# The first mixer's units in another order, with its output units begun on half of the tokens

## The reference, cut to what matters

```python
def retention_gla_mixer(h, w_in, ret_theta, gla_gk_w, gla_gk_b, gla_norm_g, s0):
    qa, ka, va, ga, qb, kb, vb, gb, lr = split_cols(h @ w_in, EVEN_SPLITS)
    ...                     # decays: from ret_theta for a, from lr for b
    o_a, ra_f, ra_b = bidir_scan(qa, ka, va, la_f, la_b, s0[0], s0[1])
    y_a = silu(ga) * merge_heads(rms_norm(o_a))
    o_b, sb_f, sb_b = bidir_scan(qb, kb, vb, ...)
    y_b = silu(gb) * merge_heads(rms_norm(o_b, gla_norm_g))
    return concatenate([y_a, y_b], axis=-1), states

# per head and direction, in chunks of 64 tokens:
#   scores = mask * (q_dec @ k_inv.T);  kv = k_end.T @ v
#   S_next = decay * S + kv;            o = scores @ v + q_dec @ S
y = y @ ev_w_out            # then gate, residual, layer norm, MLP
```

## Time and profile before

| | us |
|---|---|
| median of 3 runs (lowest, highest) | 1355.01 (1354.59, 1356.56) |
| time of the profiled execution | 1354.55 |
| its span, first to last instruction | 1352.7 |
| TensorE busy in the span | 1298.7 (96%) |
| VectorE, ScalarE, GpSimd busy | 882.6, 576.5, 102.9 |
| mean granted TensorE clock | 0.986 |

### The profile page before, as it was taken

The page is one execution under the profiler, slowest core; times in us unless marked ns, Lnnn a source line. Parts: engine busy times, 40 slices in busy tenths (PEclk is TensorE's granted clock), DMA queues, the critical chain, the costliest instruction groups (busy, mean ns, idle before and its releaser), DMA issues.

```text
span 1352.7 us, 24353 instructions
## 1 busy us (share of the span) xinstructions
PE 1298.7 (96%) x10441; PEld 1209.2 (89%) x10441; DVE 882.6 (65%) x1357; ACT 576.5 (43%) x889; POOL 102.9 (8%) x153
## 2 busy tenths in 40 slices
PE   5899999999999999899999999999999899899997
PEld 4799999899898778699999898898999899899997
DVE  3567755566463355568677587676787886667566
ACT  4433446544673435516522313313155665435431
POOL 0111110000001111000000011111100110000000
PEclk8899999999999999899999999999999999999999
DMA  9897886455244454023435456475444201455550
GB/s 350 300 331 235 260 255 183 115 173 160 89 152 153 169 169 144 1 94 125 141 125 172 125 172 188 152 246 180 148 132 156 63 1 54 164 189 190 187 184 32
DMA packets 163881, 218.40 MB, mean 161 GB/s; under 512 B 6030, under 2 KB 141589, under 8 KB 163638
## 3 DMA queue, kind: packets, MB, share of 16 engines
q1 hardware_dynamic: 140196, 148.11, 33.6%
q0 software_dynamic: 22880, 67.42, 15.9%
q10 hardware_dynamic: 698, 1.32, 0.3%
HBM read 215.70 MB, written 1.12 MB: 160 GB/s over the span
## 4 chain that ended last, share of the span: by engine, by line
PE 83%; DVE 7%; ACT 4%; DMA 3%; issue 2%; POOL 0%; SPq 0%; DVEq 0%; ACTq 0%
PE bank L1314 29%; PE bank L692 10%; PE bank L711 10%; PE bank L744 7%; PE bank L727 4%; PE bank L1391 2%; PE bank L1221 2%; PE bank L885 2%; PE bank L803 2%; PE bank L1406 2%; DVE wlo L2068 1%; PE bank L1292 1%; DMA strip_b<-distance_parts 1%; DMA graw_b<-in_w_mod 1%; PE bank L1148 1%
## 5 line engine op out<-in xcount | busy, mean ns | idle before, releaser
L2068 DVE TENSOR_TENSOR wlo<-raw,whi 128x2048 fp32r<-128x2048 f32 x131 | 297.3, 2274 | 95.0 <-ACT whi L1485 94.4
L1485 ACT ACTIVATE whi<-raw 128x2048 fp32r<-128x2048 f32 x131 | 248.0, 1899 | 194.0 <-PE bank L1314 130.7
L1314 PE MATMUL bank<-whi,m_hi 128*128 128x256 f32 x576 | 160.3, 278 | 1.2 <-DVE m_lo L2663 0.8
L1314 PE MATMUL bank<-whi,m_lo 128*128 128x256 f32 x576 | 159.7, 277 | 0.0
L1314 PE MATMUL bank<-wlo,m_hi 128*128 128x256 f32 x576 | 159.7, 277 | 0.0
L1314 PE MATMUL bank<-a_hi,whi 128*128 128x256 f32 (+1 forms) x448 | 148.6, 332 | 0.0
L1314 PE MATMUL bank<-a_lo,whi 128*128 128x256 f32 (+1 forms) x448 | 148.2, 331 | 0.0
L1314 PE MATMUL bank<-a_hi,wlo 128*128 128x256 f32 (+1 forms) x448 | 147.9, 330 | 0.0
L1314 PEld LDWEIGHTS bank<-whi,m_hi 128*128 128x128 f32 x576 | 108.6, 188 | 1.9 <-DVE m_lo L2663 1.2
L1314 PEld LDWEIGHTS bank<-wlo,m_hi 128*128 128x128 f32 x576 | 108.1, 188 | 0.1
L1314 PEld LDWEIGHTS bank<-whi,m_lo 128*128 128x128 f32 x576 | 108.3, 188 | 0.0
(11 more groups left out here) (437 smaller groups left out, 3338.2 us busy)
## 6 DMA issues: line engine op xcount, KB each, us to landing
raw<-in_mlp_w SPq DMA_DIRECT2D x64, 1024.0 KB, 5.2
raw<-in_w_in SPq DMA_DIRECT2D x32, 1024.0 KB, 7.3
graw_b<-in_w_mod POOLq DMA_DIRECT2D x64, 512.0 KB, 4.8
raw<-in_ev_w_in SPq DMA_DIRECT2D x12, 1024.0 KB, 5.1
pre<-in_w_ada SPq DMA_DIRECT2D x16, 512.0 KB, 10.0
graw_a<-in_w_mod POOLq DMA_DIRECT2D x16, 512.0 KB, 7.1
Y<-in_w_mod POOLq DMA_DIRECT2D x16, 512.0 KB, 4.2
raw<-in_od_w_qkv SPq DMA_DIRECT2D x6, 1024.0 KB, 4.8
```

The source lines that it names most:

```text
L1314: mm = nc.tensor.matmul(o, x, y, start=(k == 0 and i == 0), stop=(k == KT - 1 and i == 2))
L1485: nc.scalar.activation(split_pair(u, kt * cols)[0], landing(u, kt * cols), ACT.Copy).then_inc(hi_done, 1)
L2068: nc.vector.tensor_tensor(split_pair(u, n)[1], landing(u, n), bf(whi[u % HI], n), ALU.subtract).then_inc(lo_done, 1)
```

## The change

The units' columns come in another order: E+7 and E+8 are now the retention queries and keys, E+9 and E+11 the retention values, E+10 and E+12 the retention gates. Each head's pair of waits (scores to sums, sums to out) now has one tile in it, heads 6 and 7 too: E+11's second tile and E+12's two are left for them. `gy_turn` now turns two column blocks for one token half, `gy_turn(0)` and `(1)` for the first 256 tokens, `(2)` and `(3)` for the rest, and uses banks 7, 0, 7, 6; the first two stand between E+12's tiles, and `evo_tile(0)` starts before `head_out(7)`. `take_mod` stands ahead of `split_lo` in VectorE's list. Two gates (`GATE_TILE`) get a wait of their own, since their unit now comes late. The root of the first four heads (`head_roots(0)`, a Sqrt) comes before two Silu units instead of after all of them, and one small Sqrt is added ahead of the second. All else is the same set of instructions in another order.

```diff
-        for c0 in (1536, 1792, 2048, 2304, 2560, 2816, 1024, 0, 256, 512, 1280, 768):
+        for c0 in (1536, 1792, 2048, 2304, 2560, 2816, 0, 256, 512, 1024, 768, 1280):
...
-        MIX_V = {U_EV + 4: 256, U_EV + 10: 0, U_EV + 12: 256}
-        MIX_G = {U_EV + 5: 512, U_EV + 6: 768, U_EV + 7: 0, U_EV + 11: 256}
-        MIX_QT, MIX_KT = U_EV + 8, U_EV + 9
+        MIX_V = {U_EV + 4: 256, U_EV + 9: 0, U_EV + 11: 256}
+        MIX_G = {U_EV + 5: 512, U_EV + 6: 768, U_EV + 10: 0, U_EV + 12: 256}
+        MIX_QT, MIX_KT = U_EV + 7, U_EV + 8
...
+        GATE_TILE = {4: before[U_EV + 10] + 1, 6: before[U_EV + 12] + 1}
+        GY_BANK = (7, 0, 7, 6)
...
-        ROW_BANKS = {2: (0, 1), 3: (0, 1), 4: (4, 5, 6, 7), 5: (4, 5), 6: (6, 7)}
+        ROW_BANKS = {2: (6, 1), 3: (7, 2), 4: (4, 5, 6, 7), 5: (4, 5), 6: (6, 7)}
...
```

The parts of the diff in ScalarE's and VectorE's lists that the prediction speaks of:

```diff
+            gemv_take(15)
+            split_hi(E + 13)
+            head_states(4)
             mix_take(E + 10, 0)
-            head_squares(3)
...
             mix_take(E + 12, 1)
+            head_states(7)
+            nc.scalar.activation(stat[:, 61:62], stat[:, 40:41], ACT.Sqrt)
+            take_rows(2)
+            take_rows(3)
             split_hi(E + 16)
...
+                if hd in GATE_TILE:
+                    taken(dve, GATE_TILE[hd])
...
-            split_lo(E + 10)
-            take_mod(12)
             head_gate(1)
             head_scores(2)
-            split_lo(E + 11)
-            take_mod(13)
+            take_mod(12)
+            split_lo(E + 10)
             head_states(2)
...
-            for h in range(2):
-                ret_decays(h)
+            ret_decays(0)
             head_gate(3)
+            ret_decays(1)
+            split_lo(E + 12)
+            take_mod(14)
...
+            gy_low(0)
+            head_scores(7)
+            gy_low(1)
+            split_lo(E + 15)
             head_gate(6)
             head_states(7)
             split_lo(E + 16)
```

More of the change, by code:

```diff
@@ L391, in build @@
         FILLS = 6
-        MIX_V = {U_EV + 4: 256, U_EV + 10: 0, U_EV + 12: 256}
-        MIX_G = {U_EV + 5: 512, U_EV + 6: 768, U_EV + 7: 0, U_EV + 11: 256}
-        MIX_QT, MIX_KT = U_EV + 8, U_EV + 9
+        MIX_V = {U_EV + 4: 256, U_EV + 9: 0, U_EV + 11: 256}
+        MIX_G = {U_EV + 5: 512, U_EV + 6: 768, U_EV + 10: 0, U_EV + 12: 256}
+        MIX_QT, MIX_KT = U_EV + 7, U_EV + 8
         GLA_V0 = (place[U_EV + 3, 0], place[U_EV + 3, 1])
-        V_TILES = {0: GLA_V0, 2: (before[U_EV + 4], before[U_EV + 4] + 1), 4: (before[U_EV + 10], before[U_EV + 10] + 1),
-                   6: (before[U_EV + 12], before[U_EV + 12] + 1)}
+        V_TILES = {0: GLA_V0, 2: (before[U_EV + 4], before[U_EV + 4] + 1), 4: (before[U_EV + 9], before[U_EV + 9] + 1),
+                   6: (before[U_EV + 11], before[U_EV + 11] + 1)}
+        GATE_TILE = {4: before[U_EV + 10] + 1, 6: before[U_EV + 12] + 1}
+        GY_BANK = (7, 0, 7, 6)
         KV_OUT = 10
@@ L1169, in _, with gy_turn @@
             mix_tile(E + 5, 1)
-            mix_tile(E + 6, 0)
             head_out(0)
             head_scores(1)
+            mix_tile(E + 6, 0)
+            head_sums(1)
             mix_tile(E + 6, 1)
-            head_sums(1)
-            mix_tile(E + 7, 0)
-            mix_tile(E + 7, 1)
             head_out(1)
             head_scores(2)
-            mix_tile(E + 8, 0)
+            mix_tile(E + 7, 0)
             head_sums(2)
-            mix_tile(E + 8, 1)
+            mix_tile(E + 7, 1)
             head_out(2)
             head_scores(3)
+            mix_tile(E + 8, 0)
+            head_sums(3)
+            mix_tile(E + 8, 1)
+            head_out(3)
             mix_tile(E + 9, 0)
-            head_sums(3)
+            head_scores(4)
             mix_tile(E + 9, 1)
+            head_sums(4)
             mix_tile(E + 10, 0)
[L1188 to L1193, removed]
             head_out(4)
             head_scores(5)
-            mix_tile(E + 12, 0)
+            mix_tile(E + 10, 1)
             head_sums(5)
-            mix_tile(E + 12, 1)
+            mix_tile(E + 11, 0)
             head_out(5)
+            head_scores(6)
+            mix_tile(E + 11, 1)
             assert gq[0] == U_Q
[L1202 to L1210, removed]
+            head_sums(6)
+            def gy_turn(i):
+                if i == 0:
+                    pe.wait_ge(y_scaled, 1)
+                    pe.wait_ge(mod_done, B_LOOP)
+                elif i == 1:
+                    taken(pe, before[U_EV + 12])
+                for kk in range(2):
+                    for m in range(2):
+                        c0 = (4 + 2 * (i % 2) + kk) * P
+                        mm = nc.tensor.transpose(bank[GY_BANK[i]][:, kk * S + m * P:kk * S + (m + 1) * P],
+                                                 gy[:, 2 * (i // 2) + m, c0:c0 + P], ident)
                 mm.then_inc(ey_t, 1)
@@ L1225, in evo_tile @@
                     mm.then_inc(tile_done, 1)
[L1227 to L1233, removed]
+            mix_tile(E + 12, 0)
+            gy_turn(0)
+            head_out(6)
             head_scores(7)
-            head_out(6)
+            gy_turn(1)
+            mix_tile(E + 12, 1)
             head_sums(7)
-            pe.wait_ge(ey_lo, 4)
+            pe.wait_ge(kir_done, 2 * RH)
+            taken(pe, before[U_EV + 12] + 1)
             gate_rows((M0C + 16,), ROW_BANKS[2])
-            evo_tile(2, range(4, KT))
[L1240 to L1245, removed]
+            pe.wait_ge(ey_lo, 1)
+            pe.wait_ge(sc_done, 2 * RH)
+            gate_rows((M0 + 16,), ROW_BANKS[3])
+            pe.wait_ge(ey_lo, 2)
+            evo_tile(0, range(4, KT))
+            head_out(7)
+            pe.wait_ge(rowb_done, 2)
+            evo_tile(1, range(4, KT))
+            pe.wait_ge(rowb_done, 3)
+            gy_turn(2)
+            gy_turn(3)
+            evo_tile(2, range(4, KT))
             pe.wait_ge(gy_done, 2 * RH)
@@ L1706, in mix_take @@
                     if u > U_EV + 4:
-                        act.wait_ge(o_mm, 2 if u == U_EV + 10 else 4)
+                        act.wait_ge(o_mm, 2 if u == U_EV + 9 else 4)
                     nc.scalar.activation(vv[:, 2 * i:2 * i + 2, MIX_V[u]:MIX_V[u] + UC],
@@ L1789, in gy_high @@
                 act.wait_ge(ey_t, i + 1)
-                nc.scalar.activation(a_hi[:, 4 + i, :], bank[i % 2][:, :], ACT.Copy, scale=gg).then_inc(ey_hi, 1)
+                ks, ts = slice(4 + 2 * (i % 2), 6 + 2 * (i % 2)), slice((i // 2) * S, (i // 2 + 1) * S)
+                nc.scalar.activation(a_hi[:, ks, ts], bank[GY_BANK[i]][:, :].rearrange("p (k t) -> p k t", k=2), ACT.Copy, scale=gg)\
+                    .then_inc(ey_hi, 1)
             E = U_EV
@@ L1808, in _ @@
             split_hi(E + 9)
-            mix_take(E + 6, 0)
             head_squares(0)
             head_rows(1)
+            mix_take(E + 6, 0)
+            head_states(1)
             mix_take(E + 6, 1)
             gemv_take(12)
-            head_states(1)
             split_hi(E + 10)
+            head_squares(1)
+            head_rows(2)
             mix_take(E + 7, 0)
+            head_states(2)
             mix_take(E + 7, 1)
             gemv_take(13)
-            head_squares(1)
-            head_rows(2)
@@ L1821, in _ @@
             split_hi(E + 11)
[L1822 to L1825, removed]
             head_squares(2)
             head_rows(3)
+            head_states(3)
+            gemv_take(14)
             split_hi(E + 12)
-            head_states(3)
+            head_squares(3)
+            spread_queries(trB[0], 1).then_inc(q_wide, 1)
+            head_roots(0)
+            mix_take(E + 9, 0)
+            head_rows(4)
+            mix_take(E + 9, 1)
@@ L1830, in _ @@
             gemv_take(15)
             split_hi(E + 13)
+            head_states(4)
             mix_take(E + 10, 0)
-            head_squares(3)
+            head_squares(4)
+            head_rows(5)
             mix_take(E + 10, 1)
             gemv_take(16)
-            head_rows(4)
-            spread_queries(trB[0], 1).then_inc(q_wide, 1)
+            head_states(5)
             split_hi(E + 14)
             mix_take(E + 11, 0)
-            head_states(4)
+            head_squares(5)
+            head_rows(6)
@@ L1841, in _ @@
             mix_take(E + 11, 1)
             gemv_take(17)
-            head_roots(0)
-            head_squares(4)
-            head_rows(5)
+            head_states(6)
             split_hi(E + 15)
             mix_take(E + 12, 0)
-            head_states(5)
+            gy_high(0)
+            head_squares(6)
+            head_rows(7)
+            gy_high(1)
             mix_take(E + 12, 1)
+            head_states(7)
+            nc.scalar.activation(stat[:, 61:62], stat[:, 40:41], ACT.Sqrt)
@@ L1850, in _ @@
+            take_rows(2)
+            take_rows(3)
             split_hi(E + 16)
[L1851 to L1855, removed]
+            head_squares(7)
+            head_roots(1)
             gy_high(2)
             gy_high(3)
```

(43 more changed lines are left out.)

## The result

| | before | after |
|---|---|---|
| median, us (lowest to highest) | 1354.8 (1354.42 to 1356.56) | 1337.8 (1335.22 to 1340.16) |
| span of the profiled execution | 1352.7 | 1338.4 |
| mean granted clock | 0.986 | 0.991 |

The ratio is 0.9871, with a 95% interval from 0.9851 to 0.9892: faster by 1.3%, 17.5 us, where 15.2 were forecast. The sign and the mechanism were right; the sum was too small.

What follows compares the result with a forecast made beforehand. TensorE's idle time and low clock in the mixer bound the kernel. Of 16.1 us removable, less 0.6 for quarters and 0.3 for ties, 15.2 us are saved: 1339.8 us, range 1337.5 to 1346.5.

Steps and rivals of the forecast that it cites:

- What bounds the kernel: TensorE, 96% busy, loses 12.2 us idle and 5.5 us to low clock in the mixer; later work should just move forward.
- The walk: Check of each new wait in the mixer against row durations: other engines' chains fit under TensorE's work, some by 0.3 us.
- The three ties at heads 2, 4 and block 14: Places where other engines finish about when TensorE needs them: 0.1 us each, 0.3 in all, up to 1.5 if late.
- The two added table loads: ScalarE's two more loads of 1.28 us, behind the states of heads 4 and 7: cost 0, at most 2.6 us.
- The sum: Whole saving forecast: 16.1 us less 0.6 for quarters and 0.3 for ties, 15.2 us.
- The deductions: Waits kept in the mixer: 0.6 us for late quarter loads and 0.3 us for ties, taken off the removable time.
- The 16.1 us that can be had: TensorE's removable loss in the mixer: 10.6 us of idle time, leaving 1.6 for `a_lo`, plus 5.5 us of clock.
- The clock term: Low clock in the mixer: 4.3 us in `head_out(6)`, `head_sums(7)` and `gate_rows`, and 1.2 us at 448 us.
- (a): Rival: one mixer tie becomes a wait with low clock, 6.7 to 11.2 us saved, 1344 to 1348 us; chance 0.16.
- (b): Rival: MLP loads waiting for `head_out(7)` set the pace after 606 us, swallowing the saving, 1353 to 1355 us; chance 0.05.
- (c): Rival: states' chain outgrows its tile at heads 1 to 7, 3.1 us each, 22 us lost, 1361 us; chance 0.06.
- The quarters: GpSimd refills of about 2 MB at 258 GB/s, about 8 us, against 8.3 us spacing: 0.3 us kept at each of two places.

Runs made afterwards that it cites:

- e1: The changed kernel run once more with no edit: 1338.4 us, ratio 0.9869 to the kernel before.
- e4: The changed kernel with `take_mod` behind `split_lo` again for blocks 11, 12 and 13: 1340.0 us, ratio 0.9885 to the kernel before.
- e2: The changed kernel with the first token half's last four transposes put ahead of `evo_tile(3, range(4, KT))`: 1336.0 us, ratio 0.9851 to the kernel before.
- e5: The kernel before with only `take_mod(12)` moved ahead of `head_states(1)` on VectorE: 1351.6 us, ratio 0.9976 to the kernel before.
- e6: The kernel before with transposes of a constant filling TensorE's waits for heads 6 and 7: 1351.5 us, ratio 0.9972 to the kernel before.
- e7: The changed kernel with three extra VectorE operations (0.7 us each) in the states of heads 1 to 7: 1363.9 us, ratio 1.0069 to the kernel before.
- e8: The changed kernel with `mix_tile(E + 12, 0)` moved ahead of `head_sums(6)` and 46 constant transposes in the resulting wait: 1344.5 us, ratio 0.9923 to the kernel before.
- e3: The changed kernel with `mix_tile(E + 12, 0)` moved ahead of `head_sums(6)`, leaving head 6's wait uncovered: 1348.8 us, ratio 0.9939 to the kernel before.

## Why the prediction was right or wrong

**What bounds the kernel: right.** Idle time and clock of TensorE in the mixer were the whole of it, and the rest of the program moved forward unchanged.

**The walk: right, point by point.** No `head_out` waits in the profile after. The three ties at heads 2, 4 and block 14 came out at 0.0 us. `take_mod(12)` was done 1.9 us into its tile (forecast: within 3). The two added table loads are there, of 1.28 us each; no wait on TensorE names them, and the two Sqrts began 0.01 us behind the loads at 487.22 and 562.42 us. `second_half` began 172.6 us after the quarters of E+5, against 174.4 by the forecast (590.5 - 416.1).

**The sum: 1.8 us too small in the profile after, and this is the step that failed.** It forecast 15.2 us, and the stretch shows 17.0 (16.4 in e1, and 17.2 in e4, which differs only in the place of the split). Two terms were mis-sized.
- The deductions, 0.6 for the quarters and 0.3 for the ties. Measured were 0.2, 0.8, 0.5 and 0.0 us for the quarters in four profiles with this order (after, e1, e2, e4), and nothing for the ties. That is 0.7 us of the error in the profile after.
- The 16.1 us that can be had. I added the listed waits and the clock of four pieces. The idle time fell by 10.4 us, as summed (12.2 to 1.8), so the other 17.0 - 10.4 = 6.6 us stand against my 5.5. The missing 1.1 us are work that ran slowly and that I did not count. 0.4 of it is the pair of quarters at 447 us, 1.40 us in place of 1.00, which e5 restored. For the other 0.7 I have only the restart behind a wait. It took 0.2 to 0.3 us in e2, and before two groups of 16 products right behind waits were long too, where they take 1.09 us elsewhere:

```profile
557.31 1.18 PE bank L1136 x16
...
562.10 1.16 PE bank L1123 x16
```

That this adds up to 0.7 us is argued, not shown, and the cause of that part stays open. The clock term itself, 4.3 us in the tail, was right to 0.2 us: e6 gave 4.1, because `gate_rows` took 1.98 us there and not the 1.78 of the sum. So the open part is nearer 0.9 than 0.7 us.

**The range** was cut too close at its good side. "Every term at its good end" left out what the list of waits does not hold, and runs of the changed kernel alone spread from 1335.2 to 1340.2 us.

**The rivals.** (a) and (b) did not happen. (c) would have been as dear as said or dearer, 20.2 / 7 = 2.9 us per head in the profile of e7 and 27 / 7 = 3.9 by its median, against 3.1, but the change does not do it. In the profile after VectorE's states end only 0.25 us (head 2, 460.33 to 460.58) to 1.33 us (head 5) before `head_out` begins, so one short operation on VectorE in the wrong place spends the cover.

**The quarters.** The row's 258 GB/s was the better guide: the refills that TensorE met took 7.2 to 7.7 us in the profiles of before, after and e1, and at the spacing of 8.3 us the waits for them came to 0.8 us at most. By the 341 GB/s that the Trainium skill gives ("DMA: Bandwidth & Descriptors", Bandwidth) nothing would have been late; the trace after has 0.2 us and e5 2.4 us. The 6.15 us for 1 MB in the same row of that page are half of that rate, so the prediction's 6.2 us for 2 MB follow from the one figure and not from the other.

## What to carry to other kernels

Take the longest dependent chain over the engines that do not bound the kernel (here 6.1 us from sums to out) and see that each pass of it has one piece of the bounding engine's work of that length or more; walked from rows of the trace, it put three ties within 0.1 us. Price a wait of the matrix engine not at its length alone: the clock behind one near 2 us can cost more than the wait (3.2 us behind 1.88 and 4.6 behind 2.05 in e7). Where it can't be covered by real work, idle transposes into free columns bring the clock's share back (4.1 us in e6, 4.5 in e8).

## What the runs showed of the hardware

**The clock can fall without an idle moment.** In the window 365 to 375 us, ahead of all that any kernel here changes, TensorE is busy throughout; its last listed wait, 0.8 us, ended at about 350 us. The granted clock there is 0.83 or 0.84 in four of ten profiles (after, e1, e2, e4), 0.90 in one and 1.00 in five. First the kernel e1 (the same code as after), then e3, whose code is the same up to there:

```profile
365.00:375.00 10.00, 10.00 (x50) 7.67 (x49) 1.10 (x1) 7.88 (x14) 0.00 (x0) 0.83 0.48 151
```

```profile
365.00:375.00 10.00, 10.00 (x63) 7.67 (x62) 0.62 (x1) 8.34 (x15) 0.00 (x0) 1.00 0.41 133
```

Fifty products against 63 in the same ten us. What TensorE did before it were full tiles and two groups that fill little of the array: 24 products with 32 output rows (L1056) and 8 with 33 input rows (L1081). In the profile after, the low clock went on into the next window (375 to 385: 0.82). There `head_sums(0)` began at 413.36 us, 3.4 us later than in e1. This is one source of the differences between runs of one kernel; how much of them it makes up is not known. Whether these two groups bring it was not tried.

**Two waits of the same length can end differently.** In e7 the clock fell at 2 of 7 waits: it fell behind one of 1.88 us and not behind one of 1.86, so the length alone does not tell them apart.
